# An expert-layer kernel on one core: gate and up columns loaded as 8 KB rows, four gate banks before four up banks

## What is computed

```python
def swiglu(h, w_gate_up, w_down):
    g, u = jnp.split(h @ w_gate_up, 2, axis=-1)
    return (jax.nn.silu(g) * u) @ w_down
...
    for e in range(N_EXPERTS):
        y = y + gates[:, e:e + 1] * swiglu(xt, w_gate_up[e], w_down[e])
```

## Time and profile before

| what | us |
|---|---|
| median of 3 runs (1111.07 to 1112.01) | 1111.94 |
| the profiled execution | 1111.86 |
| its span | 1109.8 |
| TensorE busy in the span | 1072.9 (97%) |
| VectorE, ScalarE busy | 618.5, 525.1 |
| DMA | 341.93 MB in the main queue, 309 GB/s over the span |

### The profile page before, as it was taken

The page is one execution under the profiler, slowest core; times in us unless marked ns, Lnnn a source line. Parts: engine busy times, 40 slices in busy tenths (PEclk is TensorE's granted clock), DMA queues, the critical chain, the costliest instruction groups (busy, mean ns, idle before and its releaser), DMA issues.

```text
span 1109.8 us, 15850 instructions
## 1 busy us (share of the span) xinstructions
PE 1072.9 (97%) x5798; PEld 801.1 (72%) x5798; DVE 618.5 (56%) x674; ACT 525.1 (47%) x589; POOL 90.2 (8%) x150
## 2 busy tenths in 40 slices
PE   9999999999999999999998999998999998999994
PEld 9887888888899888887456887355887354888341
DVE  6865645455654557995017995117896106897102
ACT  6555544344435656773016774015775015775001
POOL 2100000000000006980000000000000000000000
PEclk9999999999999999999999999999999999999998
DMA  9933566555454336997999999999999999999994
GB/s 348 365 124 114 190 185 195 172 191 206 153 179 163 114 115 220 378 361 280 391 417 409 402 418 406 392 419 409 401 419 409 398 417 409 403 416 409 386 412 185
DMA packets 110935, 343.46 MB, mean 309 GB/s; under 512 B 11614, under 2 KB 38283, under 8 KB 100619
## 3 DMA queue, kind: packets, MB, share of 16 engines
q1 hardware_dynamic: 110714, 341.93, 81.1%
q10 hardware_dynamic: 144, 0.52, 0.1%
HBM read 341.37 MB, written 1.05 MB: 309 GB/s over the span
## 4 chain that ended last, share of the span: by engine, by line
PE 82%; DMA 7%; DVE 5%; SPq 2%; ACT 2%; issue 1%; POOL 0%; POOLq 0%; DVEq 0%; ACTq 0%
PE ps L1578 21%; PE ps L1573 20%; PE ps L1575 19%; PE ps L1574 19%; DMA raw<-moe_w_gate_up_dram 5%; DMA raw<-moe_w_down_dram 2%; SPq L382 2%; PE ps L1950 1%; DVE wlo L1070 1%; DVE h L1354 1%; ACT whi L659 1%; DVE wlo L1068 1%; DVE wlo L1081 1%; DMA raw<-mla_w_down_dram 1%; PE ps L1994 1%
## 5 line engine op out<-in xcount | busy, mean ns | idle before, releaser
L659 ACT ACTIVATE whi<-raw 128x2048 fp32r<-128x2048 f32 (+2 forms) x203 | 341.4, 1688 | 223.6 <-PE ps L1575 201.7
L1081 DVE TENSOR_TENSOR wlo<-raw,whi 128x2048 fp32r<-128x2048 f32 x151 | 346.5, 2299 | 111.0 <-ACT whi L659 110.6
L1573 PE MATMUL ps<-whi,xhi 128*128 128x512 f32 (+3 forms) x688 | 263.5, 383 | 9.2 <-DVE wlo L1081 8.5
L1575 PE MATMUL ps<-wlo,xhi 128*128 128x512 f32 (+3 forms) x688 | 259.4, 377 | 0.0
L1574 PE MATMUL ps<-whi,xlo 128*128 128x512 f32 (+3 forms) x688 | 259.0, 376 | 0.0
L1573 PEld LDWEIGHTS ps<-whi,xhi 128*128 128x128 f32 x688 | 129.6, 188 | 35.7 <-issue 7.7
L1578 PE MATMUL ps<-raw,xs 128*64 128x512 f32 (+2 forms) x1024 | 155.0, 461 | 0.0
L1575 PEld LDWEIGHTS ps<-wlo,xhi 128*128 128x128 f32 x688 | 129.3, 188 | 23.8
L1574 PEld LDWEIGHTS ps<-whi,xlo 128*128 128x128 f32 x688 | 129.5, 188 | 22.2
L1578 PEld LDWEIGHTS ps<-raw,xs 128*64 128x64 f32 x1024 | 68.3, 137 | 81.7 <-issue 71.5
L1573 PE MATMUL ps<-whi,hhi 128*128 128x512 f32 x264 | 106.0, 401 | 0.0
(11 more groups left out here) (329 smaller groups left out, 1046.7 us busy)
## 6 DMA issues: line engine op xcount, KB each, us to landing
raw<-moe_w_gate_up_dram SPq DMA_DIRECT2D x256, 512.0 KB, 13.9
raw<-moe_w_down_dram SPq DMA_DIRECT2D x80, 1024.0 KB, 17.8
raw<-moe_w_gate_up_dram SPq DMA_DIRECT2D x96, 384.0 KB, 9.5
raw<-ffn_w_gate_up_dram SPq DMA_DIRECT2D x44, 512.0 KB, 4.9
raw<-ffn_w_down_dram SPq DMA_DIRECT2D x22, 512.0 KB, 4.4
raw<-kv_shared_w_dram SPq DMA_DIRECT2D x16, 512.0 KB, 3.9
raw<-moe_w_gate_up_dram SPq DMA_DIRECT2D x32, 256.0 KB, 9.8
raw<-moe_w_down_dram SPq DMA_DIRECT2D x16, 512.0 KB, 18.4
```

Of the source, the lines that this page charges most:

```text
L659: return nc.scalar.activation(o, i, ACT.Copy, scale=scale)
L1081: V.tensor_tensor(wlo[:, s, :].rearrange("p a w -> p (a w)"), raw[:, (hh // 2) % RAW, :], whi[:, s, :].bitcast(F32).rearrange("p a w -> p ...
L1573: pe.matmul(o, a_hi, b_hi, start=start, stop=False, skip_group_check=True)
L1575: return pe.matmul(o, a_hi, b_lo, start=False, stop=stop, skip_group_check=True)
```

## The change

Units 0 to 15 of every item become one transfer each of 2048 neighbouring columns: units 0 to 7 the gate columns of row chunks 0 to 7, units 8 to 15 the up columns. A big item then fills gate banks 0 to 3 in units 0 to 7 and up banks 4, 5, 7 and 6 in units 8 to 15. SiLU of groups 0 to 3 stands in steps 7 to 9 of ScalarE, the gates in steps 15 to 17 of VectorE, the steps of `HIDDEN_AT` are 18, 19, 20, 22, 24 and 26, and big items transpose into bank 3 instead of 6. `gm`, which keeps SiLU results, gets four buffers in place of two; to make room, constants of the attention stages move to addresses that the expert layer covers. A small item fills banks 0 and 2 with gate and 1 and 3 with up columns, works units 16 to 21 in banks 5 and 7, and does its first transposes after units 17 and 19. The core of the diff:

```diff
 def sub_bank(j):
 
-    return (0, 2, 4, 7, 2, 1)[j]
+    return (0, 1, 2, 3, 0, 2)[j]
 
 
 def up_bank(j):
-    return (1, 3, 5, 0, 3, 1)[j]
+    return (4, 5, 7, 6, 1, 2)[j]
 
 
 SMALL_GROUPS = 4
 SMALL_WIDTH = (512, 512, 256, 128)
 SMALL_FIRST = (0, 512, 1024, 1280)
-SMALL_END = (8, 16, 22, 22)
+SMALL_END = (8, 8, 22, 22)
+SMALL_BANKS = (0, 2, 5, 7)
 TR_BANK = 6
-HIDDEN_AT = (10, 12, 18, 20, 24, 26)
+BIG_TR_BANK = 3
+HIDDEN_AT = (18, 19, 20, 22, 24, 26)
 
 
 def segments(x):
 
     if x < 16:
-        return [(a * 1024, x % 8, a, x // 8 * 1024, 1024) for a in range(2)]
+        return [(0, x % 8, x // 8, 0, 2048)]
...
+        hhi, hlo, xm, gm, sel, selT, selN, each = over(
             ("hhi", [P, 2 * GA, SEQ], F32R), ("hlo", [P, 2 * GA, SEQ], F32R),
-            ("xm", [P, TC, D], F32), ("gu", [P, 2, TC, GW], F32), ("sel", [P, TC, P], F32),
-            ("selT", [P, SEQ], F32R), ("xs", [P, KD, SMALL], F32), ("selN", [P, SEQ], F32R))
+            ("xm", [P, TC, D], F32), ("gm", [P, 4, 512], F32), ("sel", [P, TC, P], F32),
+            ("selT", [P, SEQ], F32R), ("selN", [P, SEQ], F32R), ("each", [P, 2 * TC, ITEMS, N_EXP], F32))
+        gu, xs = over(("before_gu", [P, 8192], F32), ("gu", [P, 2, TC, GW], F32), ("gm_2", [P, 512], F32), ("xs", [P, KD, SMALL], F32))[1::2]
...
             def big(i, g, following):
 
                 def silu(j):
-                    if j % 2 == 0:
-                        act.wait_ge(even_done, i * 3 + j // 2 + 1)
+                    if j == 4:
+                        act.wait_ge(even_done, i + 1)
                     else:
-                        act.wait_ge(used, i * FH + H_MOE + 2 * (8, 16, GU)[j // 2])
-                    if j >= 2:
-                        act.wait_ge(gu_tr[2], i * SUB + j - 1)
+                        act.wait_ge(used, i * FH + H_MOE + 2 * (8 if j < 4 else GU))
+                    if j >= 4:
+                        act.wait_ge(gu_tr[2], i * SUB + j - 3)
                     w = sub_width(j)
-                    nc.scalar.activation(gm[:, j % 2, 0:w], ps[:, sub_bank(j), 0:w], ACT.Silu).then_inc(silu_done[2], 1)
+                    nc.scalar.activation(gm[:, j % 4, 0:w], ps[:, sub_bank(j), 0:w], ACT.Silu).then_inc(silu_done[2], 1)
 
                 def high(j):
                     act.wait_ge(gu_tr[2], i * SUB + j + 1)
                     w = sub_width(j)
-                    copy(ehi[:, 4 * j:4 * j + w // P, :].rearrange("p a s -> p (a s)"), ps[:, TR_BANK, 0:w]).then_inc(h_hi[2], 1)
+                    copy(ehi[:, 4 * j:4 * j + w // P, :].rearrange("p a s -> p (a s)"), ps[:, BIG_TR_BANK, 0:w]).then_inc(h_hi[2], 1)
 
                 for x in range(2, FU):
-                    if x in (7, 15, 21):
-                        silu({7: 0, 15: 2, 21: 4}[x])
+                    if x in (7, 8, 9, 21):
+                        silu({7: 0, 8: 2, 9: 3, 21: 4}[x])
                     if x in HIDDEN_AT:
                         high(HIDDEN_AT.index(x))
...
                     if x + 3 < FU or following == "big":
                         split_high_unit(H_MOE + RING + 2 * x, i, g)
-                    if x in (7, 15, 21):
-                        silu({7: 1, 15: 3, 21: 5}[x])
+                    if x in (7, 21):
+                        silu({7: 1, 21: 5}[x])
...
                     w = SMALL_WIDTH[j]
-                    nc.scalar.activation(gm[:, j % 2, 0:w], ps[:, (0, 2, 0, 1)[j], 0:w], ACT.Silu).then_inc(small_silu, 1)
+                    nc.scalar.activation(gm[:, j % 2, 0:w], ps[:, SMALL_BANKS[j], 0:w], ACT.Silu).then_inc(small_silu, 1)
 
                 def hidden(j):
                     act.wait_ge(small_tr, p * SMALL_GROUPS + j + 1)
                 for j in range(2):
                     silu(j)
+                for j in range(2):
                     hidden(j)
                 silu(2)
...
                 def gate(j):
                     dve.wait_ge(silu_done[2], i * SUB + j + 1)
+                    if j == 0:
+                        dve.wait_ge(used, i * FH + H_MOE + 32)
                     w = sub_width(j)
                     up = ps[:, up_bank(j), :] if j < SUB - 1 else ps[:, up_bank(j), w:2 * w]
-                    V.tensor_tensor(gm[:, j % 2, 0:w], up, gm[:, j % 2, 0:w], ALU.mult).then_inc(gated[2], 1)
+                    V.tensor_tensor(gm[:, j % 4, 0:w], up, gm[:, j % 4, 0:w], ALU.mult).then_inc(gated[2], 1)
 
                 def low(j):
                     dve.wait_ge(h_hi[2], i * SUB + j + 1)
                     w = sub_width(j)
                     chunks = slice(4 * j, 4 * j + w // P)
-                    V.tensor_tensor(elo[:, chunks, :].rearrange("p a s -> p (a s)"), ps[:, TR_BANK, 0:w],
+                    V.tensor_tensor(elo[:, chunks, :].rearrange("p a s -> p (a s)"), ps[:, BIG_TR_BANK, 0:w],
                                     ehi[:, chunks, :].bitcast(F32).rearrange("p a s -> p (a s)"), ALU.subtract).then_inc(h_lo[2], 1)
 
                 for x in range(2, FU):
-                    if x in (7, 15, 21):
-                        gate({7: 0, 15: 2, 21: 4}[x])
+                    if x in (15, 16, 17, 21):
+                        gate({15: 0, 16: 2, 17: 3, 21: 4}[x])
                     if x in HIDDEN_AT:
                         low(HIDDEN_AT.index(x))
...
-                    if x in (7, 15, 21):
-                        gate({7: 1, 15: 3, 21: 5}[x])
+                    if x in (15, 21):
+                        gate({15: 1, 21: 5}[x])
...
                 def gate(j):
                     dve.wait_ge(small_silu, p * SMALL_GROUPS + j + 1)
                     w = SMALL_WIDTH[j]
-                    up = ps[:, 2 * j + 1, :] if j < 2 else ps[:, j - 2, w:2 * w]
+                    if j == 0:
+                        dve.wait_ge(small_used, p * FU + 16)
+                    up = ps[:, 2 * j + 1, :] if j < 2 else ps[:, SMALL_BANKS[j], w:2 * w]
                     V.tensor_tensor(gm[:, j % 2, 0:w], up, gm[:, j % 2, 0:w], ALU.mult).then_inc(small_gated, 1)
 
-                gate(0)
                 item_gates(g)
                 if following is not None:
                     choose(g + 1, following)
-                for j in range(1, SMALL_GROUPS):
+                for j in range(SMALL_GROUPS):
                     gate(j)
                 if following == "big":
...
                 if x < 16:
-                    k = x % 8
+                    k, a = x % 8, x // 8
                     if x < 8:
                         pe.wait_ge(xe_lo, i * KD + k + 1)
                     if x == 8:
                         pe.wait_ge(h_ready[4], g * 4 + 4)
-                    for n in range(2):
-                        j = 2 * (x // 8) + n
-                        for a in range(2):
-                            if k == 0 and j == 3 and a == 1:
-                                pe.wait_ge(silu_done[2], i * SUB + 1)
-                            w = slice(a * 1024 + n * 512, a * 1024 + (n + 1) * 512)
-                            last = mm3(ps[:, up_bank(j) if a else sub_bank(j), :], xhi[:, k, 0:P], xlo[:, k, 0:P],
-                                       whi_x[:, w], wlo_x[:, w], k == 0, k == KD - 1)
-                        if k == KD - 1 and n == 0:
-                            last.then_inc(even_done, 1)
+                        pe.wait_ge(selN_ready, g + 1)
+                    for j in range(4):
+                        w = slice(j * 512, (j + 1) * 512)
+                        last = mm3(ps[:, up_bank(j) if a else sub_bank(j), :], xhi[:, k, 0:P], xlo[:, k, 0:P],
+                                   whi_x[:, w], wlo_x[:, w], k == 0, k == KD - 1)
                 else:
                     if x == 16:
-                        pe.wait_ge(gated[2], i * SUB + 2)
+                        pe.wait_ge(silu_done[2], i * SUB + 4)
...
-                    for a in range(2):
+                    for j in range(2):
                         for n in range(2):
-                            w = slice(a * 1024 + n * 512, a * 1024 + (n + 1) * 512)
-                            last = mm(ps[n * SMALL:(n + 1) * SMALL, 2 * (x // 8) + a, :], xs[:, k, :], r[:, w], k == 0, k == KD - 1)
+                            w = slice(j * 1024 + n * 512, j * 1024 + (n + 1) * 512)
+                            last = mm(ps[n * SMALL:(n + 1) * SMALL, 2 * j + x // 8, :], xs[:, k, :], r[:, w], k == 0, k == KD - 1)
                 else:
                     if x == 16:
-                        pe.wait_ge(small_gated, p * SMALL_GROUPS + 1)
+                        pe.wait_ge(h_ready[4], g * 4 + 4)
                     for j in (4, 5):
                         half = sub_width(j) // 2
                         for place, k, a in pieces(x, j):
                             for n in range(2):
                                 w = slice(place + n * half, place + (n + 1) * half)
-                                last = mm(ps[n * SMALL:(n + 1) * SMALL, j - 4, a * half:(a + 1) * half], xs[:, k, :], r[:, w],
```

(34 more changed lines are left out.)

## The result

The changed kernel takes 1126.92 us (median of 4 runs, 1126.24 to 1128.95) where the kernel before takes 1111.97. The ratio is 1.0135 [1.0123, 1.0147]: 15.0 us slower, where 7.4 had been forecast and 1124.5 was the top of the range. The profiled execution took 1128.95 us, 17.1 more than the one of before.

The account below looks back on a forecast made before the run. Each pair of items was taken as a loop bounded in turn by TensorE and, from the small item's first units, by DMA. 10.8 - 1.0 - 2.4 = +7.4 us on 1111.86 gave 1119.3 us, range 1112.5 to 1124.5.

Parts of the forecast that it names:

- 1.8 had been expected: Sign looked for in the changed profile: each pair of a big and a small item about 1.8 us longer.
- Part 2: Big item's new order: TensorE idles 2.7 us before transposes(1), waiting for low(0); four items, +10.8 us (bounds +7.6 to +10.8).
- Part 3: DMA restart at the small item's unit 11: later issue into a drained queue saves 0 to 4.8 us; half taken, -2.4.
- the 1.2 and 1.8 us of queueing: Queueing of the small item's unit 11 transfers in pairs 2 and 3, which a drained queue would get back.
- 330 GB/s on average follow: Row of the kernel before: DMA's speed for 10 us after the idle queue in pair 1, though units are waiting.
- Part 1: Larger rows: 0.06 us less per unit, counting only for 17 units at handovers and the last small item: -1.0 us.
- The single transfer of 1 MB: One transfer instead of two of 512 KB at the DMA restart: between -0.5 and +1.2 us a pair, taken as 0.
- part 4: Small item: first two sets of transposes moved after units 17 and 19, and constants at other addresses, cost nothing.
- Rival A: DMA is the only bound, raw buffers absorb TensorE's stall; 112 units count, -6.7, 1105.1 us; chance 0.07.
- Rival B: No stall in the big item, as VectorE finishes low(0) in time: -1.0, 1110.9 us; chance 0.07.
- Rival C: Stall comes, but DMA restart is clean and the single transfer quicker: +3.0, 1114.9 us; within the forecast's 0.81 chance.
- Rival D: Larger rows don't become larger packets or aren't faster; the -1.0 falls away, 1120.3 us; chance 0.05.

Follow-up runs that it names:

- e1: Changed kernel with the big item's transposes alternating between banks 3 and 6, so transposes(1) no longer waits for low(0): 1112.09 us, ratio 0.9999 to the kernel before.
- e6: Changed kernel with 11 unneeded multiplications of the identity on TensorE ahead of the wait of transposes(1): 1122.21 us, ratio 1.0108 to the kernel before.
- e4: Kernel before with one number of HIDDEN_AT changed, 20 to 19, so transposes(3) stands one unit early and waits: 1125.93 us, ratio 1.0128.
- e5: Changed kernel with two transpose banks and units 0 to 15 again as two 512 KB transfers (4 KB rows): 1112.05 us, ratio 1.0003 to the kernel before.
- e2: Changed kernel with units 0 to 15 again as two 512 KB transfers each (4 KB rows): 1127.84 us, ratio 1.014 to the kernel before.
- e7: Changed kernel with two transpose banks and five small units instead of two before the big item's scatter: 1107.35 us, ratio 0.9959 to the kernel before.
- e9: Changed kernel with two transpose banks, five small units before the scatter and 4 KB rows again: 1111.36 us, ratio 0.9997 to the kernel before.
- e8: Kernel before with five small units instead of two before the big item's scatter: 1110.81 us, ratio 0.999.

## Why the prediction was wrong

**Direction and mechanism: right.** The stall sits where it was put, before transposes(1), ended by low(0), four times, 10.7 us in all where +10.8 was the term; VectorE's order of work is the one that was built from the old rows. e1 shows that nothing else in the change costs time that can be told. A pair, taken from one handover's end to the next, is 5.6 and 4.4 us longer than before, where 1.8 had been expected.

**Part 2, the step that failed.** "After it nothing more is late" and "Four big items: +10.8 us" price a stall as its idle time. The runs showed a second part: TensorE's granted clock falls around the end of the stall and is at 1.2 GHz in the stretch behind it, while TensorE has work without a gap. It costs 1.5 to 1.7 us where it happens: 4.9 in the profile, 3.0 to 4.7 by e6. In the sum the term would have stood at 10.8 + 4.9 = 15.7. No row of before had such a stall inside a big item, so the clock was 1.00 in all rows read. That was carried over to a kernel with other stalls, and the term for the clock stood at nothing without a reason. The wait of 1.54 us at the handover would not have warned of it: in the trace of before the matmuls behind it stand 0.23 us apart. Behind the 1.9 us of e4 they don't in three of four cases.

**Part 3, the credit of -2.4: not given.** With the clock's 4.9 added the sum is 10.8 - 1.0 + 4.9 = 14.7 without any credit, 12.3 with it. Measured were 15.0 by the medians and 17.1 in the profiled execution, from which the 4.9 is read; the waits for `wlo` at the handovers grew by 1.1 instead of shrinking. And e4, where no transfer changed, lost its stalls in full as well. The stream did start late, with an empty queue in all four pairs, but then stuttered as in the earlier trace rows; the "330 GB/s on average follow" row, already in hand, was the better guide than the 1.2 and 1.8 us of queueing. Half a credit was a middle between ends, not a reading of the nearest row.

**Part 1, the rows, -1.0: not to be told from 0.** e1 against e5 gives 0.0, the changed kernel against e2 -0.9 (-0.6 by the ratios); both within their intervals. That not all 112 units are bound by DMA (-6.7) was right for this kernel; 17 of them and none can't be told apart. And e7 against e9 shows how it depends on the rest: with the small units moved ahead the same rows are worth 4.0 us. The speed of the rows was as read: 420 or 421 GB/s where 4 KB rows had 410, 2.4% again.

The Trainium skill ("DMA: Bandwidth & Descriptors", Why small descriptors are slow) leads to 1.2% by its fixed cost of a packet, as an estimate; the rows of after show twice that, as those of before did.

**The single transfer of 1 MB, 0, and part 4, 0:** nothing in the runs speaks against it; e2 against the changed kernel holds both the rows and the number of transfers, and moves the time by less than 1 us together.

**Rival A (DMA the only bound), 0.07:** refuted by e4, where the buffers absorbed none of the stall. **Rival B (no stall):** did not come, but e1 is its case made real; 1110.9 had been worked out for it, 1112.09 was measured, with its row term of -1.0 not to be seen. **Rival C:** refuted by the stutter. **Rival D:** the rows are faster, so it is false in its reason, though its missing microsecond can't be told.

**The range** ended at 1124.5, though the ends of the terms reached +14.6 (1126.5). Even that was short of the measured 1126.92, since the clock was in none of them.

Left open: why the stream stutters after an empty queue, with 4 KB rows and 8 KB rows alike, and what decides in one item that the clock falls and in the next, after the same idle time, that it doesn't.

## What to carry to other kernels

Price a new stall of TensorE as its idle time plus what the clock may take behind it. Look for the clock's part not in the busy share but in the granted clock and the number of matmuls of the windows after the stall; 2.7 us idle cost 3.9 on average here. Faster transfers pay little where the stream then waits for buffers: first free the buffers that DMA waits for, then enlarge the rows (against the kernel before -4.4 us together in e7, 0 for the rows in e1, -1 for the buffers in e8). And where one bank is the reason for a wait, look whether a second is free at that moment before the order is changed: that was worth 15 us.

## What the runs showed of the hardware

- A TensorE idle of 1.9 us in the middle of dense work was followed by the lower granted clock in three of four cases (e4), one of 2.6 to 2.9 us in three of four (after) and two of four (e2). Where it fell, the windows of 5.5 us had 0.69 or 0.73 as their mean. At a handover an idle of 2.12 us was followed by the lower clock (e1), one of 2.11 us was not (after).
- Useless matmuls in the place of the idle time kept the clock: 1.00 in the windows behind all four waits of e6, worth 3.0 to 4.7 us in the end.
- A float32 multiplication of the 128 x 128 identity stands in the trace as two instructions, 40 for 20, and 20 of them took 4.5 us.
- After 2 us without a transfer, the 12 us that were read of DMA had slices of 214 and 265 GB/s between ones of 441 (after, 700 to 712 us).
